# Expert products of a mixture-of-experts layer: from split fp32r halves to plain fp32 column tiles, with 96-row items and 14 load slots

## The reference, cut to what matters

```python
T, D_MODEL, N_EXPERTS, TOP_K, MOE_D_FF = 256, 1024, 8, 2, 3584

def swiglu(x, w1, w3, w2):
    return (jax.nn.silu(x @ w1) * (x @ w3)) @ w2

def moe_swiglu(x, router_w, w1, w3, w2):
    logits = (x @ router_w).astype(F32)
    top_val, top_idx = lax.top_k(logits, TOP_K)
    top_w = jax.nn.softmax(top_val, axis=-1)
    gates = jnp.sum(jax.nn.one_hot(top_idx, N_EXPERTS, dtype=F32) * top_w[..., None], axis=-2)
    y = jnp.zeros(x.shape, F32)
    for e in range(N_EXPERTS):
        y = y + gates[..., e:e + 1] * swiglu(x, w1[e], w3[e], w2[e]).astype(F32)
    return y.astype(x.dtype)
```

## Time and profile before

| | us |
|---|---|
| median of 3 runs | 1494.49 (1493.42 to 1495.3) |
| span of the profiled execution | 1494.2 |
| PE busy | 1444.2 (97%) |
| weight loads of PE (PEld) busy | 1220.5 (82%) |
| DVE busy | 1259.3 (84%) |
| ACT busy | 1064.3 (71%) |
| POOL busy | 196.5 (13%) |
| DMA: 467.52 MB moved | mean 313 GB/s |

### The profile page before, as it was taken

The page is one execution under the profiler, slowest core; times in us unless marked ns, Lnnn a source line. Parts: engine busy times, 40 slices in busy tenths (PEclk is TensorE's granted clock), DMA queues, the critical chain, the costliest instruction groups (busy, mean ns, idle before and its releaser), DMA issues.

```text
span 1494.2 us, 21387 instructions
## 1 busy us (share of the span) xinstructions
PE 1444.2 (97%) x8114; PEld 1220.5 (82%) x8114; DVE 1259.3 (84%) x1234; ACT 1064.3 (71%) x1076; POOL 196.5 (13%) x200
## 2 busy tenths in 40 slices
PE   9999999999999999999999999999899998999997
PEld 8999899998899977877888677888676676777885
DVE  5977765566698779999989999889999999999994
ACT  6566533335765758788778888778888888888774
POOL 2662100000056300100101001001001001003100
PEclk9999999999999999999999999999999999999999
DMA  8562584456546339999999999999999999999990
GB/s 348 189 188 82 189 297 170 170 185 228 195 155 176 122 113 362 359 424 422 390 375 381 424 423 422 390 368 388 412 422 419 415 424 423 422 422 418 419 358 29
DMA packets 84892, 467.52 MB, mean 313 GB/s; under 512 B 16704, under 2 KB 26304, under 8 KB 30784
## 3 DMA queue, kind: packets, MB, share of 16 engines
q1 hardware_dynamic: 80816, 451.03, 76.3%
q0 software_dynamic: 3984, 15.22, 2.8%
HBM read 452.71 MB, written 13.52 MB: 312 GB/s over the span
## 4 chain that ended last, share of the span: by engine, by line
PE 60%; DVE 15%; DMA 13%; ACT 6%; issue 4%; POOL 1%; SPq 0%; DVEq 0%; ACTq 0%; POOLq 0%
DVE wlo L881 10%; DMA raw<-in_experts 8%; PE ps L2518 8%; PE ps L2519 8%; PE ps L2522 8%; PE ps L2511 7%; PE ps L2513 6%; PE ps L2512 6%; ACT whi L877 4%; PE ps L3009 3%; PE ps L3005 3%; DMA work<-in_experts 2%; PE ps L3019 2%; DMA raw<-in_stream 1%; DVE more_lo L881 1%
## 5 line engine op out<-in xcount | busy, mean ns | idle before, releaser
L881 DVE TENSOR_TENSOR wlo<-raw,whi 128x2048 fp32r<-128x2048 f32 x373 | 848.6, 2302 | 59.4 <-ACT whi L877 57.3
L877 ACT CAST whi<-raw 128x2048 fp32r<-128x2048 f32 x373 | 708.1, 1913 | 83.2 <-DMA raw<-in_experts 75.4
L2518 PE MATMUL ps<-whi,xh 128*128 128x512 f32 (+3 forms) x588 | 227.3, 388 | 1.3 <-DVE xl L1695 0.5
L2519 PE MATMUL ps<-whi,xl 128*128 128x512 f32 (+3 forms) x588 | 224.3, 383 | 0.0
L2511 PE MATMUL ps<-xh,whi 128*128 128x256 f32 x656 | 187.1, 285 | 0.0
L2513 PE MATMUL ps<-xh,wlo 128*128 128x256 f32 x656 | 184.1, 281 | 0.0
L2512 PE MATMUL ps<-xl,whi 128*128 128x256 f32 x656 | 184.1, 281 | 0.0
L2522 PE MATMUL ps<-wlo,xh 128*128 128x512 f32 (+3 forms) x588 | 154.4, 384 | 0.7 <-DVE wlo L881 0.6
L3009 PE MATMUL ps<-wlo,xh 128*128 128x512 f32 x464 | 132.5, 408 | 13.7 <-DVE wlo L881 12.7
L2518 PEld LDWEIGHTS ps<-whi,xh 128*128 128x128 f32 x588 | 110.4, 188 | 26.3 <-ACT whi L877 1.6
L3005 PE MATMUL ps<-whi,xh 128*128 128x512 f32 x464 | 131.1, 404 | 0.1
(11 more groups left out here) (420 smaller groups left out, 2046.3 us busy)
## 6 DMA issues: line engine op xcount, KB each, us to landing
raw<-in_experts SPq DMA_DIRECT2D x288, 1024.0 KB, 10.0
raw<-in_stream SPq DMA_DIRECT2D x85, 1024.0 KB, 5.5
work<-in_experts SPq DMA_DIRECT2D x48, 1024.0 KB, 9.7
y_rows<-work POOLq DMA_DIRECT2D x1, 4096.0 KB, 18.6
m_rows<-work SPq DMA_DIRECT2D x2, 768.0 KB, 4.4
work<-x_inv_rows SPq DMA_DIRECT2D x2, 768.0 KB, 5.5
work<-xt_rows SPq DMA_DIRECT2D x2, 768.0 KB, 7.6
y_rows<-work POOLq DMA_DIRECT2D x1, 1280.0 KB, 22.5
```

What stands on the lines that cost most here:

```text
L877: nc.scalar.copy(upper_slot(n), landed_slot(n)).then_inc(s_hi, 1)
L881: nc.vector.tensor_tensor(lower_slot(n), landed_slot(n), upper_slot(n).bitcast(F32), ALU.subtract).then_inc(s_lo, 1)
L2518: pe.matmul(out, xu, wu, start=start, stop=False)
L2519: return pe.matmul(out, xd, wu, start=False, stop=False)
```

## The change

- Whole items hold 96 rows (`WIDE`), not 128. Every expert may now have up to three extra items; the largest number of extra items, over all routings, is 6, not 5.
- Expert slots are not split. TensorE reads the landed fp32 slot itself (`unsplit`), in plain fp32 matmuls. Only the stream's slots and the four gate slots at the end are split as before.
- A small item's product of 512 moving columns is two matmuls of 256 with 64 stationary columns each, one for each half of the array's columns (`small_products`; for C two of 512). A whole item's is six matmuls with 32 stationary columns: three of 384 moving columns on column strips 0 to 2, for 32 rows each, and three of 128 moving columns on strip 3 (`whole_products`).
- `merge`, the pair forms, and the split of the activations are gone; small and whole items run the same `rest_of_item`.
- The items' ring is 14 slots: the landed and the upper copy's place of each of the 6 ring positions, and two in the work area. C slots are counted as used half by half as A and B are.
- The last two items are a whole one (`third`) and a small one (`last`), where they were small and whole. The scatter matrix is 64 rows high. `last_down`, which had interleaved the last C products with the scatter, is gone; the gate slots are split after the last item.

The core of the diff:

```diff
+WIDE, GROUP = 96, 32
-ROUND_PHASE = {"to_whole": PAIRS, "to_small": PAIRS, "small": RUN, "turn": TURN, "last": LAST}
+ROUND_PHASE = {"to_whole": PAIRS, "to_small": PAIRS, "small": RUN, "turn": TURN, "third": TURN, "last": LAST}
-ITEM_RING, ITEM_LEAD = 7, 5
+ITEM_RING = 14
...
-    ring_of_items = [(n_stream + k) % RING for k in range(RING)] + [RING]
+    freed = [(n_stream + k) % RING for k in range(RING)]
+    ring_of_items = [slot for k in freed[:4] for slot in (k, RING + k)] + [2 * RING, 2 * RING + 1]
+    ring_of_items += [slot for k in freed[4:] for slot in (k, RING + k)]
...
         def landed_slot(n):
-            return raw[:, slot_of(n), :] if slot_of(n) < RING else part(SPARE, SLOT)
+            n = slot_of(n)
+            if n < 2 * RING:
+                return (raw if n < RING else upper)[:, n % RING, :]
+            return part(SPARE + SLOT * (n - 2 * RING), SLOT)
+        def unsplit(key, start, width):
+            return landed_slot(load_at[key])[:, start:start + width]
...
             for n in range(n_stream, n_before + ITEM_RING):
-                if slot_of(n) == RING and n < n_stream + ITEM_RING:
+                if slot_of(n) >= 2 * RING and n < n_stream + ITEM_RING:
                     sp.wait_ge(s_hn, NB)
...
-                nc.vector.tensor_scalar(room, busy_rank, NS - 0.5, float(HALF), ALU.is_gt, ALU.mult).then_inc(st.sem, st.up())
+                nc.vector.tensor_scalar(room, busy_rank, NS - 0.5, float(WIDE - HALF), ALU.is_gt, ALU.mult).then_inc(st.sem, st.up())
...
+            def small_products(key, rows, w, width, start, stop):
+                for side in range(2):
+                    ins = pe.matmul(bank(key, 0, width)[HALF * side:HALF * side + HALF], rows, w[:, width * side:width * side + width],
+                                    start=start, stop=stop)
+                return ins
+
+            def whole_products(key, rows, w, start, stop):
+                for g in range(3):
+                    pe.matmul(bank(key, 0, 384)[GROUP * g:GROUP * g + GROUP], rows(g), w[:, 0:384], start=start, stop=stop)
+                for g in range(3):
+                    ins = pe.matmul(bank(key, P * g, P)[WIDE:P], rows(g), w[:, 384:512], start=start and g == 0, stop=stop and g == 2)
+                return ins
+
+            def up(kind, ph, j, whole, now=None):
                 key = (kind, ph, j)
                 opened(key, now)
                 for half in range(2):
-                    upper_ready(pe, key + (half,), now)
+                    landed(pe, load_at[key + (half,)], now)
                     for q in range(4):
                         k = 4 * half + q
-                        pe.matmul(bank(key), x_pair[:, k, :], weights(key + (half,), 512 * q, 512)[0], start=k == 0, stop=False)
-                    ready(pe, key + (half,), now)
-                    for q in range(4):
-                        k = 4 * half + q
-                        ins = pe.matmul(bank(key), x_pair[:, k, :], weights(key + (half,), 512 * q, 512)[1], start=False,
-                                        stop=k == KC - 1)
+                        w = unsplit(key + (half,), 512 * q, 512)
+                        if whole:
+                            ins = whole_products(key, lambda g: x_wide[:, k, GROUP * g:GROUP * g + GROUP], w, k == 0, k == KC - 1)
+                        else:
+                            ins = small_products(key, x_small[:, k, :], w, T, k == 0, k == KC - 1)
                     ins.then_inc(s_fill if half else s_used, 1)
...
-            rounds = pe.value_load(table[0:1, NI:NI + 1], min_val=NS - 1 - PAIRED, max_val=NS - 1 - PAIRED + MORE)
+            rounds = pe.value_load(table[0:1, NI:NI + 1], min_val=NS - 2 - PAIRED, max_val=NS - 2 - PAIRED + MORE)
             with pe.Fori(0, rounds) as r:
-                rest_of_small("small", Now(RUN, r))
-            rest_of_small("turn", Now(TURN, rounds))
-            rest_of_item("last", Now(LAST, rounds))
+                rest_of_item("small", Now(RUN, r))
+            rest_of_item("turn", Now(TURN, rounds))
+            rest_of_item("third", Now(TURN, rounds))
+            items = Now(LAST, rounds)
+            rest_of_item("last", items)
+            last_ple(items)
```

More of the change, by code:

```diff
@@ L41, in most_extra_items, with fewest @@
 def most_extra_items():
-    return max(f + s + t + u for f in range(T // HALF) for s in range(NS) for t in range(NBIG + 1) for u in range(t + 1)
-               if (f * HALF + 1 if f else 0) + (HALF + 1) * (s + (NBIG - t if s else 0)) + (P + 1) * t + HALF * u <= T * TOPK)
+    def fewest(extra, room):
+        return room + HALF * (extra - 1) + 1 if extra else 0
+    most = 0
+    for first, small, *whole in itertools.product(range(T // HALF), range(NS), *[range(T // HALF)] * NBIG):
+        least = HALF + 1 if small else 0
+        rows = [fewest(first, HALF)] + [least] * small + [max(least, fewest(extra, WIDE)) for extra in whole]
+        if sum(rows) <= T * TOPK and max(rows) <= T:
+            most = max(most, first + small + sum(whole))
+    return most
 MORE = most_extra_items()
@@ L278, in ple_tiles, with whole_now, whole_next, first_gather_tiles @@
             turn_tiles(t, 3, [(c, c) for c in EARLY])
[L281 to L291, removed]
+def whole_now(ph):
+    return ph in WHOLE
+def whole_next(ph):
+    return AFTER.get(ph) in WHOLE
+def first_gather_tiles(t):
+    for half in range(2):
+        t.add(("GA", "first", half), 2 + half, "a")
+def gather_tiles(t, ph):
+    for half in range(2 if whole_next(ph) else 1):
+        t.add(("GA", ph, half), (7, 5)[half], "a")
 def scatter_tiles(t, m):
@@ L422, in plan_loads, with group @@
         add((kind, 1), ("PP", 1, 1, 1), behind=("LG",))
[L424 to L428, removed]
+    def group(ph, j):
+        for kind in "AB":
+            add((kind, ph, j, 0), (kind, ph, j), signal=True)
+            add((kind, ph, j, 1), (kind, ph, j))
     def down(ph, j):
-        tile = ("B", ph, j + 1)
-        if small_now(ph):
-            tile = ("B", ph, j + 2) if j < NJ - 2 else ("TT", ph, NJ - 1)
+        done = ("YY", ph, 1 if whole_now(ph) else 0)
         for half in range(2):
-            until_tile = ("YY", ph, half) if j == NJ - 1 else tile
-            behind = ("B", ph, 0) if j == NJ - 1 and ph != "last" else None
-            add(("C", ph, j, half), until_tile, signal=j < NJ - 1 or half == 0, behind=behind)
+            add(("C", ph, j, half), done, signal=j < NJ - 1 or half == 0)
     def rest_of_item(ph):
@@ L1602, in rest_of_item @@
[L1602 to L1613 removed]
+                    filled(act, ("YY", ph, 0), now)
@@ L1631, in _ @@
             turned_residual(5, LATE, items)
-            split.behind(("YY", "last", 1), items)
+            for n in range(n_gates + 2, n_gates + 4):
+                split_upper(n, items)
             act.wait_ge(s_rstd, 6)
@@ L2416, in _ @@
-            split.behind(("B", "first", 0))
+                    product(ph, 0, whole_next(ph), now)
+                    return
+                step()
+                filled(dve, ("YY", ph, 0), now)
+                dve.wait_ge(s_yw, through(items_before[ph] + 16, now, "rows"))
+                nc.vector.tensor_copy(ysb[0:HALF, 512:D], bank(("YY", ph, 0))[HALF:P]).then_inc(s_free["v"], 1)
+                for n in range(n_gates, n_gates + 2):
+                    split_lower(n, now)
+                for m in range(2):
+                    for b in range(NB):
+                        add_to_residual(("SC", b, m), b, m, now)
```

794 lines of the change are left out of this document (255 added, 539 removed).

## The result

The changed kernel takes 1574.87 us (median of 4 runs, 1570.77 to 1579.37) against 1494.89 us (1493.42 to 1501.45) of the kernel before in the same runs: ratio 1.0534 [1.0502, 1.0565], 5.3% slower. The forecast was 1553 us, in a range of 1535 to 1615: the direction and the cause hold, the point is 22 us low.

The account below looks back on a forecast made before the run. From 543 to 1445 us the kernel was taken as bound by expert-weight bytes, some 5% lost to TensorE, splits and a short ring. Forecast 1553 us: 107 for the ninth item, less 44 of stretch, less 4 of tail; range 1535 to 1615.

Parts of the forecast that it names:

- the ninth item: Expert loads: 114 tokens exceed 96 rows, so the busiest expert gets an extra small item, 42 more slots, costing 107 us.
- Rival 1: Expert items: the busiest expert has 96 tokens or fewer, so 8 items and 1446 us; chance 5%.
- TensorE's price: Expert products in plain fp32 column tiles: some 115 us for a whole item, some 75 for a small one.
- Rival 3: Whole items: four strips overlap only in part, 140 to 220 us an item, 1560 to 1800 us in all; chance 9%.
- rival 2: Whole items: strips start in issue order, each record holding back later ones, 257 us an item, 1910 us; chance 6%.
- The splits and the slots: Expert stretch: dropping the splits and using 14 load slots brings it to 421 GB/s, 44 us less.
- Start: First expert load: issued at 543.03 us as before; eight at once close the low-rate gap, 2 to 6 us lost if late.
- Bytes: Expert stretch: 362.2 MB of before, less 2 MB of gates, plus 44.0 and 1.0 MB for the extra item.
- Rate: Expert stretch: all of it runs at 421 GB/s; 417 to 425 would give +9 or -9 us.
- 14 slots: Load ring: loads run on 32 us while TensorE is late, so a whole item costs nothing up to about 138 us.
- The tail: After the last expert load: 13 us to the first gate product, then 31.7; together 45 us (40 to 53).
- the sum itself: Whole kernel: the terms hold as added, 1553 us, between 1535 and 1590; chance 80%.

Follow-up runs that it names:

- experiment 1: The changed kernel with one comparison changed so that the busiest expert gets no extra item (its last 18 tokens left out): 1465.97 us, ratio 0.9801.
- experiment 2: The kernel before with only the room of whole items cut to 96 rows, old products, splits and ring, nine items: 1600.47 us, ratio 1.0714.
- experiment 5: The changed kernel with all expert loads but the first eighteen cut to half, so TensorE sets the pace: 1417.7 us, one run.
- experiment 3: The changed kernel with the busiest expert's item at 128 rows in full-width plain fp32, no strips there, 8 items: 1472.87 us, ratio 0.9868.
- experiment 4: The changed kernel with all three whole items at 128 rows in full-width plain fp32, no strips, 8 items: 1496.04 us, ratio 1.001.
- experiment 10: The changed kernel with the busiest expert at 128 rows full width, additions ahead of the gate splits and four filler products at the end: 1471.12 us, ratio 0.9847.
- experiment 7: The changed kernel again, unedited, on the same chip as other follow-up runs: 1576.59 us, ratio 1.0521.
- experiment 8: The changed kernel with small items' products cut into pieces of 128 columns, about 2.7 times as many TensorE instructions there: 1580.3 us, ratio 1.0564.
- experiment 6: The changed kernel with 7 load slots for the items instead of 14: 1583.99 us, ratio 1.0573.

## Why the prediction was right, and where it was off

**What bounds it, and the ninth item: right.** 378 loads, DMA share 1.01, and experiments 1 and 2 put 109 (105.8 in the stretch of the loads) and 106 us on the item that was reckoned at 107. Rival 1 (no ninth item, 1446 us) is out; built as experiment 1 it gives 1466, 20 over its sum for the reasons below.

**TensorE's price: right on unseen ground.** Whole item 115 reckoned, 115.6 measured; small 75 reckoned, 76.6 measured (experiment 5). The choice of 0.67 us a group, from two rows of overlap with two tiles each, against 2.59 in turn, was the one that mattered most; four strips give 0.65. There was some luck in it: the two rows show 1.30 / 0.76 = 1.7 and 0.055 / 0.034 = 1.6 times the speed in turn, not 2, and by that share a whole item would have been put at 134 to 142 us. The slots hide up to about 138 of it, so the forecast would have moved by 12 us at most. Rival 3 is out. So is rival 2: a strip's second record does not hold back the first records of the others, as the lines above show. The Trainium skill's 2.38x for three column tiles ("TensorE: Matmul & The Clock Gate", Part 3), by which I estimated 145 us, is exceeded in this trace: four strips run 2.59 / 0.65 = 4.0 times as fast as in turn. The Trainium skill's rule in the same part ("MATMULs are pc-monotone in start AND end") doesn't hold here if it is read of records (1401.70 behind 1401.67 us), which is how I had priced rival 2; read of whole matmuls, the lines shown don't contradict it.

**The splits and the slots: right in kind, mis-sized.** The low rows of before are gone, but the stretch gave back 25 us where the sum had 44. The last expert load landed at 1529.3, not 1507.5. Term by term:
- Start: the first issue was at 546.2, not 543.0, 3.2 us. That is a gain and a loss together. In the profiles of the changed kernel and its variants in which the clock stood at 1.00 from 60 to 100 us (experiments 3, 4, 5 and 10) it comes at 534.2 to 538.4 us; where the clock fell to half there (0.79 over that stretch in the kernel after), at 540.3 to 546.6. Experiments 5 and 7, with the same code ahead of it and on one chip, have 535.5 and 546.6, so the low clock takes some 11 us there. Neither it nor the earlier start without it was in the sum; what brings the clock down in some executions is open.
- Bytes: the stretches sum to 408.3 MB and not 405.2, 7.4 us at 421 GB/s. I had taken off 2 MB of gate slots; in the changed kernel four stream slots are issued ahead of the last landing, where before it were two, and 44 more fetches of instructions bring 0.7 MB.
- Rate: 408.3 MB in 983.0 us is 415 GB/s. At 421, with the 2 us of first latency, it would be 971.8: 11.2 us. This is the step that was off: "The whole stretch then runs at 421 GB/s" carried over the rate of a stretch with long instructions. Before there were 62 fetches of instructions, after 106. In experiment 8 the small item between small ones has 11 more of them and takes 1.8 us more, 0.16 each; over its whole stretch it is 0.21. By these the 44 go with 7 to 9 of the 11 us, of which their own transfers are 3. The items point the same way: 14 fetches and 415 GB/s in 669 to 779 us, 1 fetch and 418 in 1104 to 1211. But the rate was high to begin with: a small item between small ones, with no or one fetch, ran at 419 to 420 GB/s in the old kernel (1128 to 1234 us, before and in experiment 2), and 418 with one fetch is still less. That part, 2 to 4 us, is open.

3.2 + 7.4 + 11.2 = 21.8 us.

**14 slots: less needed than thought.** The reckoning that a whole item costs nothing up to about 138 us held: a full-width item of 147 us costs some 10 (experiments 3 and 4), one in strips of 116 nothing that shows. Where whole items take 116, seven slots do nearly as well once the first item is in (experiment 6). The gap of 22.62 us at the start closed, which is where the further slots pay: eight loads are issued from 546.25 to 554.4, and only 546 to 559 us is under 400 GB/s.

**The tail: 48.4 against 45.** The first gate product came 14.7 us after the last landing (13 reckoned), since the second gate split ended at +10.3 and not +9.4 and the transposes ran at half clock (1.97 us for 1.03); from there it took 33.7 us, not 31.7, the clock over the tail being 0.85, where it was 0.97 before (1445 to 1494 us). I had named the clock as a danger in the small items, where it held, and not here, where TensorE stood still for 5.20 us.

**The whole:** 21.8 + 3.4 = 25 us more in the span than the sum, 1577.6 for 1552.5. The median of the runs lies 2.7 under that span and I had put it 0.5 over, which leaves the 22. The chances (0.94 slower) stood on the ninth item and were right to; the measured time lies in the 1535 to 1590 us of the sum itself, and the upper part of the range, for strips that overlap only in part, wasn't needed. That the start came out only 3.2 us late was luck: a gain and a loss that were both left out nearly cancel there.

## What to carry to other kernels

Before a tile is made smaller, ask the data how many work items that makes: one item more of 42 slots costs 106 to 109 us here, and no saving inside an item came near it (all of them together 25 us). When a kernel is bound by bytes, its sum is bytes over rate, and both want care: 1% of rate is 10 us, and many short instructions went with nearly that much here. A deep ring lets a heavy item (147 us against 108 of bytes) pass at a quarter of its excess, some 10 us, when a light one follows, which is a way to keep the large tile for the one expert that needs it.

## What the runs showed of the hardware beyond what was expected

- Four column strips with plain fp32 overlap fully: 0.65 us for a group that in turn would be 2.59; the records of one strip do not wait for those of another.
- A fetch of TensorE's instructions (16 KB) goes with 0.16 to 0.21 us less of loading, four to five times its bytes' worth and two to three times its own transfer's (0.07 us); a whole item in strips has 14 of them, one small item has 1.
- The clock stayed at 0.98 to 1.00 in the small items, where TensorE waits some 22 of 107 us in short pieces, and fell to 0.50 in the tail, where it stood still in one piece before the transposes (5.20 us).
- At 60 to 100 us the clock falls in some executions of the same code and not in others (0.79 and 1.00), and the first expert load comes 11 us later with it (546.6 against 535.5 us).
- A load lands 27.5 us after its issue with 14 slots, 15.2 with 7, with items as long within 1 us from the second on.
